# Attention with the causal mask added in VectorE's copy of diagonal blocks, one full unit in four split by GpSimd, and new ranks in the planner

## The chip, the cores and the metric

One core of a Trainium2 chip. The metric is the device time of one execution in microseconds (us). Engines: TensorE (PE, its weight loads PEld), VectorE (DVE), ScalarE (ACT), GpSimd (POOL), SyncE (SP), which issues most DMAs.

## What is computed

One step of a hybrid encoder layer over 2048 prompt rows and 64 decode rows (with 128 cached keys), 8 heads of 64, all in float32:

```python
s = jnp.einsum('bqhd,bkhd->bhqk', q, k) * sc
s = s + (Fi[:, :, :, None] - Ft[:, :, None, :])      # F: running sum of log gates
s = jnp.where(kpos[None, :] <= qpos[:, None], s, -jnp.inf)
pr = jax.nn.softmax(s, axis=-1)
attn = jnp.einsum('bhqk,bkhd->bqhd', pr, v)
z = jnp.concatenate([attn * silu(ag), pool * silu(pg)], axis=-1)
y = rmsnorm(x + gate * (z @ w_out), final_g)
```

Ahead of it stand a normalization, one projection to q, k, v, gates and pooling inputs, and a pooling mixer. The last two lines above are what follows the attention.

## The kernel before

`stage_project` (to about 620 us) makes q, k, v, gates and pooling and leaves them in DRAM. `stage_finish` does the attention (620 to about 1075 us) and the output projection.

**Attention.** For each of 8 heads there are three steps: query groups c = 0 and 1 together (and the decode rows), c = 2, c = 3, where a group is 512 query rows. A step's `score` blocks are 128 query rows by up to 512 keys: TensorE makes a block by two matmuls (L1456, L1457), and for a row's last block a third, the mask (L1459), an identity times a triangular tile, both bf16. VectorE copies the block to `wts` and takes its maximum (L1571), and after a row's last block the negated maximum of the row (L1576). ScalarE takes the exponential in place, with its sum (L1528). A `unit` is 128 keys by 512 queries (fewer on the diagonal), 42 a head: `turn`, up to four fp32 transposes on TensorE (L1472); `high`, ScalarE's rounding to fp32r (L1534); `low`, VectorE's remainder (L1581); `value`, two matmuls of v with both halves (L1487). At an output's last unit ScalarE takes one half of the bank (`out`, L1542), and VectorE adds the other (`add`, L1589). A step's denominators are inverted by VectorE (`den`, L1601). In a head the outputs are c = 0, the decode rows, c = 1, 2, 3, five in all; units 0 to 3 belong to c = 0, 4 and 5 to decode, 6 to 13 to c = 1, 14 to 25 to c = 2 and 26 to 41 to c = 3. Heads run one behind the other, counted from 0.

**Rings.** Score banks 3 (`S_RING`), transpose banks 3 (`T_RING`: a bank is free after `low`), `whi` and `wlo` 6 (`W_RING`: `high` of unit i waits for `value` of unit i - 6), output banks 2. The copies of a step wait for the last transposes of two steps before.

**Order.** The instructions of TensorE, ScalarE and VectorE stand in an order that `Plan.run` writes at build time: again and again it takes the operation that can begin first by its table of costs, and by `PRIORITY` where two could begin together. Each kind keeps its own order. On the chip an engine executes its list in this order.

**Gates.** For the odd head of a pair, GpSimd multiplies each output of both heads by its gate and by the inverse denominators: `g_mul` (L1645), then `g_hi`, `g_z`, `g_lo` (L1650, L1651, L1654), four operations for each of 5 outputs. `g_mul` waits for `ag` and for `rb`, the inverse denominators of both heads repeated over partitions. These go by DRAM: `rec_out` (L1352) writes them to `rden`, `gate_in` (L1361) waits for that and loads `ag` and `rb`, two buffers each, so the third output's load waits for the first's `g_lo`. In SyncE's one queue stand between these: the load of the next head's v (it waits for the last `value` of the step before), the load of q and k of the head after next once a head's last score is made, and the stores of z (they wait for `g_lo`). GpSimd has nothing else to do in the attention:

```python
for out in OUTS:
    if out.step.e == 0: continue
...
    pool.wait_ge(rb_in[n % 2], 48 * (n // 2 + 1))
    pool.tensor_tensor(a, a, r, ALU.mult).then_inc(g_mul, 1)
    pool.wait_ge(out_ok, out.i + 1)
```

Near the end of the attention ScalarE and VectorE also split w_out in eight slices (`w_high`, `w_low`, L1563).

## Time and profile before

| | |
|---|---|
| time, median of 3 runs | 1275.52 us (1273.33 to 1277.78) |
| the profiled execution | 1271.05 us, its span 1269.3 us |
| granted clock of TensorE, mean | 0.992 |
| busy: PE, DVE, ACT, POOL | 97%, 56%, 44%, 15% of the span |
| instructions: PE, DVE, ACT, POOL | 7039, 1969, 1158, 193 |

The page gives busy times over the span, which averages stages with different limits: the projection (TensorE full, VectorE light), the attention, and the output projection. The table of busy times in short stretches separates them. In a line of the order of time, the first number is the start in us from the span's start, the second the duration, then engine, line, operation, out <- in with shapes, and in brackets the idle time of the engine before it with what ended it. Matmuls overlap in their pipeline, so the distance of two starts is their price, not their duration.

### The profile page before, as it was taken

To read this page: it belongs to the slowest core of one execution; us is meant where nothing else is said; L and a number is where in the kernel's file an instruction comes from. 1 tells how busy PE (TensorE), PEld (TensorE's weight loads), DVE (VectorE), ACT (ScalarE), POOL (GpSimd) and SP (SyncE) were. 2 spreads that over 40 slices of the span, in tenths; PEclk is the share of its full clock that TensorE was granted. 3 is DMA by queue.
4 is the path that set the end of the run, shared out by engine and by line. 5 is a ranking of instruction groups with operands and counts; after the bars stand their busy time and mean duration, and the time that the engine had idled before them with its cause. 6 is when DMAs were issued, how large, how long until landed. Compare 5 with 4: busy or idle time off the path is not lost. (4 is left out here: it accounts for less than half of the span.)

```text
span 1269.3 us, 19390 instructions
## 1 busy us (share of the span) xinstructions
PE 1229.5 (97%) x7039; PEld 1025.5 (81%) x7039; DVE 710.4 (56%) x1969; ACT 563.1 (44%) x1158; POOL 184.4 (15%) x193
## 2 busy tenths in 40 slices
PE   4899999999999999999999999999999998999997
PEld 1799988888888888888878778778787886888884
DVE  1856433334564121110069899999899998444444
ACT  3757321222121112211168789887788877101111
POOL 1433301010010000101000051032123114100000
PEclk8899999999999999999999999999999999999999
DMA  9855454022122444337175859948877965766662
GB/s 370 323 176 189 138 149 141 34 69 83 36 85 69 142 141 140 112 127 179 52 168 47 149 89 159 129 119 147 121 129 123 115 177 168 212 189 196 199 199 67
DMA packets 161893, 179.52 MB, mean 141 GB/s; under 512 B 34773, under 2 KB 124249, under 8 KB 157638
## 3 DMA queue, kind: packets, MB, share of 16 engines
q1 hardware_dynamic: 157030, 160.97, 50.9%
q10 hardware_dynamic: 4768, 17.30, 4.1%
q8 instruction: 57, 0.93, 0.4%
q14 instruction: 38, 0.31, 0.1%
HBM read 111.55 MB, written 66.69 MB: 140 GB/s over the span
## 5 line engine op out<-in xcount | busy, mean ns | idle before, releaser
L617 PE MATMUL prj_acc<-prj_hhi,til_whi 128*128 128x512 f32 (+1 forms) x800 | 285.9, 357 | 0.0
L618 PE MATMUL prj_acc<-prj_hhi,til_wlo 128*128 128x512 f32 (+1 forms) x800 | 284.8, 356 | 0.0
L619 PE MATMUL prj_acc<-prj_hlo,til_whi 128*128 128x512 f32 (+1 forms) x800 | 283.7, 355 | 0.0
L1571 DVE TENSOR_SCALAR_CACHE_REDUCE att_wts<-att_sps 128x512 f32<-128x512 f32 (+4 forms) x328 | 186.4, 595 | 89.8 <-PE att_sps L1459 88.9
L1581 DVE TENSOR_TENSOR att_wlo<-att_tps,att_whi 128x512 fp32r<-128x512 f32 (+1 forms) x336 | 183.3, 583 | 16.6 <-ACT att_whi L1534 15.9
L1534 ACT ACTIVATE att_whi<-att_tps 128x512 fp32r<-128x512 f32 (+1 forms) x336 | 160.7, 515 | 51.1 <-PE att_tps L1472 27.1
L1528 ACT ACTIVATE att_wts<-att_wts,att_nm 128x1024 f32<-128x1024 f32 (+8 forms) x200 | 175.2, 880 | 14.7 <-DVE att_nm L1576 12.6
L617 PEld LDWEIGHTS prj_acc<-prj_hhi,til_whi 128*128 128x128 f32 x800 | 150.5, 188 | 21.9
L619 PEld LDWEIGHTS prj_acc<-prj_hlo,til_whi 128*128 128x128 f32 x800 | 150.5, 188 | 21.6
L618 PEld LDWEIGHTS prj_acc<-prj_hhi,til_wlo 128*128 128x128 f32 x800 | 150.6, 188 | 21.1
L1472 PE MATMUL att_tps<-keep_ident,att_wts 128*128 128x128 f32 x1088 | 158.3, 275 | 7.0 <-DVE att_wlo L1581 5.5
L1472 PEld LDWEIGHTS att_tps<-keep_ident,att_wts 128*128 128x128 f32 x1088 | 124.6, 141 | 36.4 <-issue 18.2
L1487 PE MATMUL att_ops<-att_whi,att_vt 128*128 128x512 f32 (+1 forms) x336 | 136.0, 409 | 0.6 <-DVE att_att L1589 0.3
L1487 PE MATMUL att_ops<-att_wlo,att_vt 128*128 128x512 f32 (+1 forms) x336 | 119.5, 363 | 0.0
L977 DVE SCALAR_TENSOR_TENSOR til_olo<-prj_acc,til_ohi 128x512 fp32r<-128x512 f32 (+1 forms) x40 | 23.8, 597 | 153.3 <-ACT til_ohi L800 153.3
L530 POOL TENSOR_TENSOR til_wlo<-til_wraw,til_whi 128x1024 fp32r<-128x1024 f32 x20 | 48.1, 2403 | 410.1 <-ACT til_whi L726 410.1
L1549 ACT ACTIVATE zin_junk<-zin_y 128x1024 bf16<-128x1024 f32 (+1 forms) x17 | 18.0, 1058 | 157.2 <-DVE zin_y L1615 157.2
L1645 POOL TENSOR_TENSOR att_ag<-att_ag,att_rb 128x512 f32<-128x512 f32 (+1 forms) x20 | 22.1, 1104 | 393.4 <-DMA att_rb<-scratch_rden 393.4
L1487 PEld LDWEIGHTS att_ops<-att_whi,att_vt 128*128 128x128 f32 x336 | 64.8, 193 | 8.8 <-DVE att_wlo L1581 2.1
L1487 PEld LDWEIGHTS att_ops<-att_wlo,att_vt 128*128 128x128 f32 x336 | 64.4, 192 | 4.2
L1456 PE MATMUL att_sps<-keep_ka,keep_qa 128*128 128x512 f32 (+4 forms) x164 | 65.8, 401 | 1.7 <-PEq L203 1.5
L1456 PE MATMUL att_sps<-att_ka,att_qa 128*128 128x512 f32 (+4 forms) x164 | 65.9, 402 | 0.0
(188 smaller groups left out, 1854.5 us busy)
## 6 DMA issues: line engine op xcount, KB each, us to landing
til_wraw<-in_w_in SPq DMA_DIRECT2D x20, 512.0 KB, 4.2
scratch_v<-val_vs SPq DMA_DIRECT2D x17, 512.0 KB, 4.8
val_xt<-in_x_prompt ACTq DMA_DIRECT2D x16, 512.0 KB, 4.5
ini_al<-in_w_ada SPq DMA_DIRECT2D x8, 1024.0 KB, 15.3
zin_zh<-scratch_z SPq DMA_DIRECT2D x16, 512.0 KB, 4.3
zin_zl<-scratch_z SPq DMA_DIRECT2D x16, 512.0 KB, 5.7
zin_xr<-in_x_prompt SPq DMA_DIRECT2D x16, 512.0 KB, 5.4
out_y_prompt<-zin_o ACTq DMA_DIRECT2D x16, 512.0 KB, 2.7
```

The costliest lines, as they stand in the source:

```text
L530: pool.tensor_tensor(wlo[t.n % 2][:, :, :], wraw[:, :, :], raw(whi[t.n % 2][:, :, :]), ALU.subtract).then_inc(wt_lo, 1)
L617: pe.matmul(out, w[0][:, k, :], hhi[:, k, cs], start=(k == 0), stop=False)
L618: pe.matmul(out, w[1][:, k, :], hhi[:, k, cs], start=False, stop=False)
L619: mm = pe.matmul(out, w[0][:, k, :], hlo[:, k, cs], start=False, stop=(k == KT - 1))
L977: dve.scalar_tensor_tensor(out=olo[use.slot][:, 0:x.n], in0=acc[x.i % ACC_RING][:, 0:x.n], scalar=SCALE if x.tile.kind == "Q" else 1.0, in ...
L1456: pe.matmul(bank[0:x.m, 0:x.n], qa[e][:, q], ka[e][:, k], start=True, stop=False)
L1472: mm = pe.transpose(bank[:, t * P:(t + 1) * P], weights(st, 4 * x.c + t, x.w0, P), keep["ident"][:, :])
L1487: mm = pe.matmul(bank[:, x.skip:x.width], vt[e][0:x.keys, x.tile, :], part[b][0:x.keys, x.skip:x.width], start=(x.first and part is whi), ...
L1528: act.activation(w, w, ACT.Exp, bias=nm[0:x.m, e, x.row:x.row + 1], accum_out=den[0:x.m, e, x.row, x.part:x.part + 1]).then_inc(exp_ok, 1)
L1534: act.activation(whi[x.i % W_RING][0:x.keys, x.skip:x.width], tps[x.i % T_RING][0:x.keys, x.skip:x.width], ACT.Copy).then_inc(hi_ok, 1)
L1571: dve.tensor_scalar(weights(st, x.row, x.w0, x.n), sps[x.i % S_RING][0:x.m, 0:x.n], 1.0, None, ALU.mult, ALU.max, accum_out=top[0:x.m, e, ...
L1581: dve.tensor_tensor(wlo[b][0:x.keys, x.skip:x.width], tps[x.i % T_RING][0:x.keys, x.skip:x.width], raw(whi[b][0:x.keys, x.skip:x.width]), ...
```

## The change

- The mask's matmul and its bf16 identity are gone. The mask is a float32 tile of 64 + 4 x 128 columns, zero but for two triangles, built by GpSimd behind its last normalization work of the projection. VectorE's copy of a row's last block is a `tensor_tensor_reduce` that adds a slice of it and takes the maximum.
- Of full units (no decode, nothing skipped) those with i % 4 == 3, 52 in all, are split by GpSimd: ScalarE copies the transposes as float32 to one of two new buffers `wf`, GpSimd copies these to `whi` (`p_high`) and writes the remainder to `wlo` (`p_low`); the bank is free after ScalarE. `value` waits for `p_ok`.
- GpSimd gets an order from the planner as well, in which these two and the four gate operations stand; `g_mul` is ready in the plan at the later of the output's `add` and `den` + 9 us. In the plan every GpSimd operation costs 1150 ns.
- TensorE's ranks are turn, value, score, with the score's rank by how many of the last scores are not yet copied; the costs of TensorE's matmuls are higher in the plan.

```diff
-MASKED = -1e30
+MASKED, LOWEST = -1e30, -3e38
...
-            pool.memset(keep["mask"][:, :], 0.0).then_inc(const, 1)
-            pool.affine_select(out=keep["mask"][:, :], in_=keep["mask"][:, :], compare_op=ALU.is_ge, fill=MASKED,
-            pool.wait_ge(const, 6)
-            pool.tensor_copy(keep["identb"][:, :], ident[:, :]).then_inc(const, 1)
...
+            pool.wait_ge(sq, NT)
+            pool.memset(keep["mask"][:, :], 0.0).then_inc(masked, 1)
+            pool.wait_ge(masked, 1)
+            for c0, n in ((0, DEC), (DEC + 3 * P, P)):
+                pool.affine_select(out=keep["mask"][:, c0:c0 + n], in_=keep["mask"][:, c0:c0 + n], compare_op=ALU.is_ge, fill=MASKED,
+                                   base=0, pattern=[[-1, n]], channel_multiplier=1).then_inc(masked, 1)
...
+F_UNITS = 2
+POOL_UNITS = [u.i for u in UNITS if u.i % 4 == 3 and not u.dec and not u.skip]
+GATED = [out for out in OUTS if out.step.e == 1]
+GATE_LAG = 9000
+def dve_units(i):
+    return i + 1 - sum(j <= i for j in POOL_UNITS)
...
-    PRIORITY = {"PE": ("turn", "score", "value"), "ACT": ("out", "high", "exp", "w_high"), "DVE": ("low", "add", "score", "den", "w_low")}
+    PRIORITY = {"PE": ("turn", "value", "score"), "ACT": ("out", "high", "exp", "w_high"), "DVE": ("low", "add", "score", "den", "w_low"),
+                "POOL": ("p_high", "p_low", "g_lo", "g_z", "g_hi", "g_mul")}
-        self.free = {"PE": 0, "ACT": 0, "DVE": 0}
-        self.order = {"PE": [], "ACT": [], "DVE": []}
+        self.free = {"PE": 0, "ACT": 0, "DVE": 0, "POOL": 0}
+        self.order = {"PE": [], "ACT": [], "DVE": [], "POOL": []}
-        self.tables = {"turn": UNITS, "value": UNITS, "high": UNITS, "low": UNITS, "out": OUTS, "add": OUTS, "exp": PIECES, "den": STEPS,
+        self.tables = {"turn": UNITS, "value": UNITS, "high": UNITS, "out": OUTS,
+                       "low": [u for u in UNITS if u.i not in POOL_UNITS], "p_high": [UNITS[i] for i in POOL_UNITS],
+                       "p_low": [UNITS[i] for i in POOL_UNITS], "g_mul": GATED, "g_hi": GATED, "g_z": GATED, "g_lo": GATED, "add": OUTS, "exp": PIECES, "den": STEPS,
+    def turned(self, i):
+        return self.at("high" if i in POOL_UNITS else "low", i)
+    def halved(self, i):
+        return self.at("p_low" if i in POOL_UNITS else "low", i)
...
-            return max(at("exp", LAST_PIECE[x.i]), at("low", x.i - T_RING))
+            return max(at("exp", LAST_PIECE[x.i]), self.turned(x.i - T_RING))
-            return max(at("low", x.i), at("add", x.out.i - O_RING) if x.first else 0, self.arrived(x, x.c))
+            return max(self.halved(x.i), at("add", x.out.i - O_RING) if x.first else 0, self.arrived(x, x.c))
+            if x.i in POOL_UNITS:
+                r = POOL_UNITS.index(x.i)
+                return max(at("turn", x.i), at("p_low", POOL_UNITS[r - F_UNITS]) if r >= F_UNITS else 0)
+        if kind == "p_high":
+            return max(at("high", x.i), at("value", x.i - W_RING))
+        if kind == "g_mul":
+            return max(at("add", x.i), at("den", x.step.index) + GATE_LAG)
+        if kind in ("p_low", "g_hi", "g_z", "g_lo"):
+            return at({"p_low": "p_high", "g_hi": "g_mul", "g_z": "g_hi", "g_lo": "g_z"}[kind], x.i)
...
-            mask = 50 if kind == "score" and x.last else 0
-            return 24 + 6 * x.n // 7 + mask + (80 if self.short else 0), 200
+            return 24 + 9 * x.n // 10 + (80 if self.short else 0), 200
+        if engine == "POOL":
+            return 1150, 100
...
+    def rank(self, engine, kind, x, t):
+        if engine != "PE" or kind != "score":
+            return self.PRIORITY[engine].index(kind)
+        waiting = sum(self.at("copied", i) > t for i in range(max(0, x.i - S_RING), x.i))
+        return -1 if waiting < 1 else 0.5 if waiting < 2 else 2
...
-                    key = (begin, self.PRIORITY[engine].index(kind))
+                    key = (begin, self.rank(engine, kind, table[n], begin))
-                self.short = kind == "turn" or (kind == "score" and x.last)
+                self.short = kind == "turn"
...
+def mask_of(x):
+    at = 0 if x.row == NQ else DEC + 3 * P - x.mask0
+    return slice(at, at + x.n)
...
-                    mm = pe.matmul(bank[0:x.m, 0:x.n], qb[e][:, q], kb[e][:, k], start=False, stop=not x.last)
-                    if x.last:
-                        mm = pe.matmul(bank[0:x.m, x.mask0:x.mask0 + x.m], keep["identb"][0:x.m, 0:x.m],
-                                       keep["mask"][0:x.m, 0:x.m], start=False, stop=True)
+                    mm = pe.matmul(bank[0:x.m, 0:x.n], qb[e][:, q], kb[e][:, k], start=False, stop=True)
-                    if x.i >= T_RING:
-                        pe.wait_ge(lo_ok, x.i - T_RING + 1)
+                    if x.i - T_RING in POOL_UNITS:
+                        pe.wait_ge(hi_ok, x.i - T_RING + 1)
+                    elif x.i >= T_RING:
+                        pe.wait_ge(lo_ok, dve_units(x.i - T_RING))
...
                         pe.wait_ge(v_in[e], V * (h // 2 + e))
                     if x.first and x.out.i >= O_RING:
                         pe.wait_ge(out_ok, x.out.i - O_RING + 1)
-                    pe.wait_ge(lo_ok, x.i + 1)
+                    if x.i in POOL_UNITS:
+                        pe.wait_ge(p_ok, POOL_UNITS.index(x.i) + 1)
+                    else:
+                        pe.wait_ge(lo_ok, dve_units(x.i))
                     bank = ops[x.out.i % O_RING]
                     b = x.i % W_RING
                     for part in (whi, wlo):
...
-            pe.wait_ge(lo_ok, NU)
+            pe.wait_ge(lo_ok, dve_units(NU - 1))
...
+                elif kind == "high" and x.i in POOL_UNITS:
+                    r = POOL_UNITS.index(x.i)
+                    act.wait_ge(t_full, x.i + 1)
+                    if r >= F_UNITS:
+                        act.wait_ge(p_ok, r - F_UNITS + 1)
+                    act.activation(wf[r % F_UNITS][:, :], tps[x.i % T_RING][:, :], ACT.Copy).then_inc(hi_ok, 1)
...
-                    dve.tensor_scalar(weights(st, x.row, x.w0, x.n), sps[x.i % S_RING][0:x.m, 0:x.n],
-                                      1.0, None, ALU.mult, ALU.max,
-                                      accum_out=top[0:x.m, e, x.row, x.b:x.b + 1]).then_inc(s_free, 1)
-                    if x.last:
+                    w, src, most = weights(st, x.row, x.w0, x.n), sps[x.i % S_RING][0:x.m, 0:x.n], top[0:x.m, e, x.row, x.b:x.b + 1]
+                    if not x.last:
+                        dve.tensor_scalar(w, src, 1.0, None, ALU.mult, ALU.max, accum_out=most).then_inc(s_free, 1)
+                    else:
+                        dve.tensor_tensor_reduce(w, src, keep["mask"][0:x.m, mask_of(x)], 1.0, LOWEST, ALU.add, ALU.max,
+                                                 accum_out=most).then_inc(s_free, 1)
...
-            for out in OUTS:
...
+            for kind, x in ORDER["POOL"]:
+                if kind in ("p_high", "p_low"):
+                    r, b = POOL_UNITS.index(x.i), x.i % W_RING
+                    if kind == "p_high":
+                        pool.wait_ge(hi_ok, x.i + 1)
+                        if x.i >= W_RING:
+                            pool.wait_ge(val_ok, x.i - W_RING + 1)
+                        pool.tensor_copy(whi[b][:, :], wf[r % F_UNITS][:, :]).then_inc(p_hi, 1)
+                    else:
+                        pool.wait_ge(p_hi, r + 1)
+                        pool.tensor_tensor(wlo[b][:, :], wf[r % F_UNITS][:, :], raw(whi[b][:, :]), ALU.subtract).then_inc(p_ok, 1)
+                n, cols = gates(x), x.cols
+                hi, lo = zhi[n % 2][:, 0:x.width], zlo[n % 2][:, 0:x.width]
+                a, r = ag[n % 2][:, 0:x.width], rb[n % 2][:, 0:x.width]
+                if kind == "g_mul":
+                    pool.wait_ge(rb_in[n % 2], 48 * (n // 2 + 1))
+                    pool.tensor_tensor(a, a, r, ALU.mult).then_inc(g_mul, 1)
+                elif kind == "g_hi":
+                    pool.wait_ge(out_ok, x.i + 1)
+                    pool.wait_ge(g_mul, n + 1)
+                    if n >= 2:
+                        pool.wait_ge(z_out[n % 2], 32 * (n // 2))
+                    pool.tensor_tensor(hi, a, att[:, cols], ALU.mult).then_inc(g_hi, 1)
+                elif kind == "g_z":
+                    pool.wait_ge(out_ok, x.i + 1)
+                    pool.wait_ge(g_mul, n + 1)
+                    pool.tensor_tensor(r, a, att[:, cols], ALU.mult).then_inc(g_z, 1)
+                else:
+                    pool.wait_ge(g_hi, n + 1)
+                    pool.wait_ge(g_z, n + 1)
+                    pool.tensor_tensor(lo, r, raw(hi), ALU.subtract).then_inc(g_lo, 1)
```

## Rows read from the trace of the kernel before

**Rows 1.** one stretch by engine: busy us, instructions, granted clock, DMA.

```profile
860.00:920.00 60.00, 59.30 (x364) 47.84 (x363) 55.23 (x169) 48.85 (x109) 6.79 (x6) 1.00 0.83 135
```

**Rows 2.** groups by shape, 700 to 1040 us: count, busy us, mean ns.

```profile
L1571 DVE TENSOR_SCALAR_CACHE_REDUCE att_wts<-att_sps 128x512 f32<-128x512 f32 x180 | 118.3, 681 | 0.7 <-PE att_tps L1472 0.5
L1581 DVE TENSOR_TENSOR att_wlo<-att_tps,att_whi 128x512 fp32r<-128x512 f32 x180 | 116.1, 682 | 15.5 <-ACT att_whi L1534 15.1
L1650 POOL TENSOR_TENSOR att_zhi<-att_ag,att_att 128x512 fp32r<-128x512 f32 x12 | 15.4, 1286 | 1.6
L1650 POOL TENSOR_TENSOR att_zhi<-att_ag,att_att 128x64 fp32r<-128x64 f32 x4 | 1.3, 321 | 0.5
```

**Rows 3.** TensorE in time (start us, us, line): a mask, then transposes.

```profile
805.31 0.23 PE L1459 MATMUL att_sps<-keep_mask,keep_identb 128*128 128x128 bf16 x1
805.38 0.61 PE L1472 MATMUL att_tps<-keep_ident,att_wts 128*128 128x128 f32 x4
```

**Rows 4.** VectorE in time: denominators (L1601), outputs' adds (L1589).

```profile
804.40 0.18 DVE L1601 RECIPROCAL att_rec<-att_den 128x8 f32<-128x8 f32 x1
819.04 0.69 DVE L1589 TENSOR_TENSOR att_att<-att_ops,att_tmp 64x512 f32<-64x512 f32 x1
867.34 0.70 DVE L1589 TENSOR_TENSOR att_att<-att_ops,att_tmp 64x512 f32<-64x512 f32 x1
910.22 0.18 DVE L1601 RECIPROCAL att_rec<-att_den 128x8 f32<-128x8 f32 x1
```

**Rows 5.** GpSimd in time: first gate operation, head 3's first, last output.

```profile
832.36 1.30 POOL L1645 TENSOR_TENSOR att_ag<-att_ag,att_rb 128x512 f32<-128x512 f32 x1 [45.48 <-DMA att_rb<-scratch_rden]
886.63 1.29 POOL L1645 TENSOR_TENSOR att_ag<-att_ag,att_rb 128x512 f32<-128x512 f32 x1 [24.82 <-DMA att_rb<-scratch_rden]
```

**Rows 6.** SyncE's queue in time: gate loads of the same two outputs.

```profile
826.69 0.35 SPq L1369 DMA_DIRECT2D att_ag<-scratch_ag  x1
864.08 0.34 SPq L1369 DMA_DIRECT2D att_ag<-scratch_ag  x1
```

**Rows 7.** TensorE's values: units 7, 13 of head 3; 1, 7 of head 4.

```profile
821.49 0.48 PE L1487 MATMUL att_ops<-att_whi,att_vt 128*128 128x512 f32 x1
830.15 0.40 PE L1487 MATMUL att_ops<-att_whi,att_vt 128*128 128x512 f32 x1
869.39 0.34 PE L1487 MATMUL att_ops<-att_whi,att_vt 128*128 128x384 f32 x1
875.23 0.48 PE L1487 MATMUL att_ops<-att_whi,att_vt 128*128 128x512 f32 x1
```

**Rows 8.** add and first gate operation: heads 1, 5 (last), 7 (first).

```profile
761.49 0.69 DVE L1589 TENSOR_TENSOR att_att<-att_ops,att_tmp 64x512 f32<-64x512 f32 x1
781.48 1.29 POOL L1645 TENSOR_TENSOR att_ag<-att_ag,att_rb 128x512 f32<-128x512 f32 x1 [23.62 <-DMA att_rb<-scratch_rden]
973.25 0.69 DVE L1589 TENSOR_TENSOR att_att<-att_ops,att_tmp 64x512 f32<-64x512 f32 x1
993.92 1.29 POOL L1645 TENSOR_TENSOR att_ag<-att_ag,att_rb 128x512 f32<-128x512 f32 x1 [24.00 <-DMA att_rb<-scratch_rden]
1030.78 0.69 DVE L1589 TENSOR_TENSOR att_att<-att_ops,att_tmp 64x512 f32<-64x512 f32 x1
1042.42 1.29 POOL L1645 TENSOR_TENSOR att_ag<-att_ag,att_rb 128x512 f32<-128x512 f32 x1 [43.10 <-DMA att_rb<-scratch_rden]
```

**Rows 9.** TensorE after idle near the attention's end; those 10 us.

```profile
1071.08 1.09 PE L1472 MATMUL att_tps<-keep_ident,att_wts 128*128 128x128 f32 x4 [1.81 <-DVE att_wlo L1581]
1070.00:1080.00 10.00, 8.92 (x35) 7.45 (x36) 6.82 (x9) 1.86 (x3) 1.47 (x1) 0.83 0.64 175
```

**Rows 10.** VectorE, low halves of w_out: alone, and beside a GpSimd operation.

```profile
1063.25 1.21 DVE L1563 TENSOR_TENSOR olo_w<-raw_w,ohi_w 128x1024 fp32r<-128x1024 f32 x1
1068.24 2.09 DVE L1563 TENSOR_TENSOR olo_w<-raw_w,ohi_w 128x1024 fp32r<-128x1024 f32 x1
```

**Rows 11.** GpSimd's one copy with one input, by shape.

```profile
L518 POOL CAST keep_identb<-keep_ident 128x128 bf16<-128x128 f32 x1 | 0.3, 289 | 0.1
```

More of the change, by code:

```diff
@@ L18 @@
 PAST = 128
+MASK_COLS = DEC + 4 * P
 HEADS = 8
@@ L227, in stage_project @@
             hf = a.sb("hf", [P, 2, D])
-            junk = a.sb("junk", [P, D], BF16)
+            junk = keep["junk"]
             vf = a.sb("vf", [P, 2, 512])
@@ L260, in stage_project @@
         names = ("wt_in", "wt_hi", "wt_lo", "full", "free_a", "free_d", "split_hi", "kf_ok", "m_done", "m_free", "wp_in", "wp_ok",
-                 "early_ok", "ck_in", "sp_in", "f_step", "f_exp", "f_ok", "f_hi", "f_part", "f_out",
+                 "early_ok", "masked", "ck_in", "sp_in", "f_step", "f_exp", "f_ok", "f_hi", "f_part", "f_out",
                  "d_step", "d_ok", "z_hi", "z_lo", "fill")
         (wt_in, wt_hi, wt_lo, full, free_a, free_d, split_hi, kf_ok, m_done, m_free, wp_in, wp_ok,
-         early_ok, ck_in, sp_in, f_step, f_exp, f_ok, f_hi, f_part, f_out,
+         early_ok, masked, ck_in, sp_in, f_step, f_exp, f_ok, f_hi, f_part, f_out,
          d_step, d_ok, z_hi, z_lo, fill) = (s.sem(f"t_{n}") for n in names)
@@ L575, in _ @@
             pe.wait_ge(rows_in, 80)
-            pe.wait_ge(const, 4)
+            pe.wait_ge(const, 3)
             pe.transpose(ada[0][:, 0:NROWS], rows[:, :], ident[0:NROWS, 0:NROWS]).then_inc(turned, 1)
@@ L1278, in stage_finish @@
         wlo = [s.sb(f"wlo{n}", [P, 512], F32R) for n in range(W_RING)]
+        wf = [s.sb(f"wf{n}", [P, 512]) for n in range(F_UNITS)]
         top = s.sb("top", [P, 2, NR, 4])
@@ L1294, in stage_finish @@
         names = ("s_full", "s_free", "row_ok", "exp_ok", "t_full", "hi_ok", "lo_ok", "val_ok", "low_out", "out_ok",
-                 "den_sum", "rec_ok", "g_mul", "g_hi", "g_z", "g_lo")
+                 "den_sum", "rec_ok", "p_hi", "p_ok", "g_mul", "g_hi", "g_z", "g_lo")
         (s_full, s_free, row_ok, exp_ok, t_full, hi_ok, lo_ok, val_ok, low_out, out_ok,
-         den_sum, rec_ok, g_mul, g_hi, g_z, g_lo) = (s.sem(n) for n in names)
+         den_sum, rec_ok, p_hi, p_ok, g_mul, g_hi, g_z, g_lo) = (s.sem(n) for n in names)
         rd_out, rb_in, z_out = ([s.sem(f"{n}{e}") for e in range(2)] for n in ("rd_out", "rb_in", "z_out"))
@@ L1636, in _ @@
         def _(pool):
-            for out in OUTS:
-                if out.step.e == 0:
-                    continue
-                pair, cols = out.step.pair, out.cols
-                n = gates(out)
-                hi, lo = zhi[n % 2][:, 0:out.width], zlo[n % 2][:, 0:out.width]
-                a, r = ag[n % 2][:, 0:out.width], rb[n % 2][:, 0:out.width]
-                pool.wait_ge(rb_in[n % 2], 48 * (n // 2 + 1))
-                pool.tensor_tensor(a, a, r, ALU.mult).then_inc(g_mul, 1)
-                pool.wait_ge(out_ok, out.i + 1)
-                pool.wait_ge(g_mul, n + 1)
-                if n >= 2:
-                    pool.wait_ge(z_out[n % 2], 32 * (n // 2))
-                pool.tensor_tensor(hi, a, att[:, cols], ALU.mult).then_inc(g_hi, 1)
-                pool.tensor_tensor(r, a, att[:, cols], ALU.mult).then_inc(g_z, 1)
-                pool.wait_ge(g_hi, n + 1)
-                pool.wait_ge(g_z, n + 1)
-                pool.tensor_tensor(lo, r, raw(hi), ALU.subtract).then_inc(g_lo, 1)
+            for kind, x in ORDER["POOL"]:
[9 more added lines that the diff above has]
+                        pool.tensor_tensor(wlo[b][:, :], wf[r % F_UNITS][:, :], raw(whi[b][:, :]), ALU.subtract).then_inc(p_ok, 1)
+                    continue
+                n, cols = gates(x), x.cols
[18 more added lines that the diff above has]
+                    pool.tensor_tensor(lo, r, raw(hi), ALU.subtract).then_inc(g_lo, 1)
@@ L1672, in build @@
         keep = {
-            "ident": s.sb("ident", [P, P]), "identb": s.sb("identb", [P, P], BF16), "mask": s.sb("mask", [P, P], BF16),
+            "ident": s.sb("ident", [P, P]),
             "cols": s.sb("cols", [P, NROWS]),
@@ L1676, in build @@
         }
+        with Scope(nc, "sqr") as a:
+            keep["junk"] = a.sb("junk", [P, D], BF16)
+        keep["mask"] = s.sb("mask", [P, MASK_COLS])
         with Scope(nc, "val") as a:
```

3 lines of the change are left out of this document (1 added, 2 removed).

## Prediction

> **What bounds the kernel now.** I first read the page's 40 slices: TensorE is full everywhere at full clock, and the stretch from slice 20 to slice 34 (about 620 to 1070 us, 447 us) is the attention, the only part whose work the change touches. The busy time by stretch of that stage [rows 1] shows TensorE at 59.3 of 60 us, VectorE at 55.2, ScalarE at 48.9 and GpSimd at 6.8. A busy TensorE is not a TensorE at its peak, so I compared two denominators of the same stage, VectorE's sum of row softmax to row softmax [rows 4]: from the one of head 3 (804.40) to that of head 5 (910.22) two heads take 105.8 us, 52.9 us each. VectorE is busy 92% of this, so 48.7 us a head. TensorE and VectorE are both nearly full, in queues whose order is written out by the planner: work taken from both should shorten a head. But in such queues one instruction that waits holds everything behind it, so I looked next at what GpSimd waits for. Today it does only the gates, and each time its first multiply (the line of `g_mul`) starts long after the attention output that it belongs to is there [rows 4, 5, 8]. Today nobody waits for that. This is what the prediction turns on.
>
> **Taken from TensorE: the mask matmul.** 16 rows and one decode row a head, 136 in all. The mask starts at 805.31 and the transposes behind it at 805.38 [rows 3]: 0.07 us each, and at most about 0.15 us if the long matmul behind it pays a start as well. That is 17 x 0.07 to 0.15 = 1.2 to 2.6 us a head.
>
> **Moved to VectorE: the mask in the copy.** The diagonal copies change from a scalar operation with a maximum to `tensor_tensor_reduce`. No row shows that operation. The nearest are a copy of 512 columns, 681 ns, and a tensor_tensor of 512 from PSUM and SBUF, 682 ns [rows 2]: no difference. I take nothing, as its two inputs lie where those of `low` lie. The bounds: slightly below nothing (1 us a head), if the maximum is written without an instruction of its own, and a second pass over the block: the mean diagonal block has 312 columns, 312/512 x 0.68 = 0.42 us, so 17 x 0.42 = 7 us a head more.
>
> **Taken from VectorE: the low halves of 52 units.** Units with i % 4 == 3, full and not decode, are 7 in an even head (units 7, 11, 15, 23, 27, 31, 39 of its 42) and 6 in an odd one (13, 17, 25, 29, 33, 41). Each spares a tensor_tensor of 0.68 us, some 0.6 us as they follow each other: 4 us a head of VectorE's 48.7. ScalarE is unchanged, as it writes `wf` in place of `whi`.
>
> **Added on GpSimd.** Each of the 52 units costs a copy and a subtraction. The subtraction is 1.29 us [rows 2]. The copy has no row at this size; a cast of 128 columns took 0.29 us [rows 11]. A two-input operation of 64 columns takes 0.32 and one of 512 1.29 [rows 2], so 0.18 is fixed; with that the cast's rate puts 512 columns at 0.18 + 4 x 0.11 = 0.6; the upper bound is the two-input 1.29. I take 0.6. So 52 x 1.9 = 99 us on an engine with 85% free; its load is no problem, its order is.
>
> **The order on GpSimd.** The new queue holds `p_high` and `p_low` among the gates. The planner makes `g_mul` ready at the later of the output's add and denominator + 9 us. Measured, denominator + 9 is 813.4 and the add of head 3's first output is at 819.04 [rows 4]: the add decides, and `g_mul` is put right behind it. But its `rb` rows come over DRAM: SyncE issues their load at 826.69 only [rows 6], and `g_mul` starts at 832.36 [rows 5], 28.0 us behind the denominator and 13.3 behind the add. In the new queue everything behind it stands still until then. What stands behind? The next GpSimd unit of an odd head is 13; `p_high` needs the value matmuls of unit 7 (ring of 6), which start at 821.49 [rows 7], after the add. So it can't be put ahead. Its own value matmul starts at 830.15 [rows 7]. In the new kernel it needs: 832.4 + g_mul 1.3 + the decode part's g_mul (its loads are issued behind the first's, so I put it at an end of about 835.3) + g_hi 1.3 + copy 0.6 + one gate operation between the two 1.3 + subtraction 1.3 = 840.1. TensorE stands still for **10 us**.
>
> The last output of an odd head is the same: its add is at 867.34 [rows 4], its loads are issued at 864.08 [rows 6] behind the whole q and k load of the next odd head, and `g_mul` starts at 886.63 [rows 5], 19.3 us late. Behind it stands unit 7 of the next head, which needs the value of unit 1 (869.39, again after the add) and whose value matmul starts at 875.23 [rows 7]. SyncE's chain moves by 3.4 us only. It waits for the decode part's last gate: before at 832.4 + 4 x 1.3 + 4 x 0.4 = 839.2, now at 840.1 + 1.3 + 3 x 0.4 = 842.6 (an estimate; the order of the four gate operations and the unit's two isn't shown). The landing is then at 890.0, and the value matmul can start at 890.0 + 1.3 + 1.3 + 0.6 + 1.3 + 1.3 = 895.8, in place of 875.2. The two middle outputs are less late and I give them nothing, as the next unit behind each comes later.
>
> **The sum for one pair of heads.** Denominator of head 3 to value of unit 13: 840.1 - 804.4 = 35.7 us (25.8 before). To the value of unit 7 in the next head: 895.8 - 840.1 = 55.7 us (45.1 before). From there to the next such denominator 910.22 - 875.23 = 35.0 us, less 3.6% for the lighter engines (1.9 us a head, the middle of the mask's 1.2 to 2.6, as TensorE is the fuller one), 33.7, and one restart of TensorE at the low clock. After an idle time of 1.8 us it was granted 0.83 of the clock over 10 us [rows 9], that is 3.4 us at 1.2 in place of 2.4 GHz and 1.7 us of work lost. Sum 35.7 + 55.7 + 33.7 + 1.7 = 126.8 us against 105.8: **21 us more a pair**. The pairs of heads 1 and 2, and 5 and 6, have the same lateness (last output 20.0 and 20.7 us) [rows 8]; I take the same 21 for each. Head 7 has only the first: 11.6 us late [rows 8], so 8.3 + 1.7 = 10 us. Head 0 and the rest of head 7 gain 3.6% of some 80 us, 3 us. The end costs 2 us (below). Sum 3 x 21 + 10 - 3 + 2 = 72 us. The profiled run took 1271.05 us (its span is 1269.3), the median of the three is 1275.5, 4.5 above. 1275.5 + 72 gives **1347 us**.
>
> **At the end of the attention** the eight low halves of w_out, VectorE reading two SBUF inputs, run beside GpSimd: 1.21 us alone, 2.09 us beside a GpSimd operation [rows 10]. Head 7's last units 29, 33 and 41 add six GpSimd operations there: at most 6 x 0.9 = 5 us, partly beside other work; I took 2. The Trainium skill says in SBUF: State Buffer, Who interferes with whom, that a VectorE instruction with two SBUF inputs and a GpSimd one that reads SBUF exclude each other, the later blocking fully, and that one SBUF input doesn't contend. The trace agrees with the first (2.09 against 1.21). By it the masked copy, with PSUM and one SBUF input, doesn't slow. The sum is the same by the row.
>
> **Edits that cost nothing.** The mask is built later on GpSimd, two selects and a fill, under 2 us at a point where that engine waits for ScalarE for most of the projection; if this cover were gone it would cost these 2 us. The bf16 identity goes. The ranks of the plan let score matmuls wait when two scores are not yet copied; a step's copies wait for the transposes of two steps before, so denominators can't come much earlier, and a later one only makes the gates later.
>
> **The rivals.** (a) *No blocking*, the gates' loads are there in time. Then a head goes from 52.9 to about 51.0 us, as TensorE loses 1.9 and VectorE 4: 8 x 1.9 = 15 us, **1260 us**, faster. For it: both full engines get lighter. Against it: lateness of 11.6 to 20.7 us [rows 8] and four more such places, on a chain of SyncE and DMA that the change leaves alone. It decides if the loads land within some 2 us of the add. Chance 0.17. (b) *Half the blocking*: DMA queues run emptier while TensorE waits, or the order saves one of the two units: 36 us, **1311 us**. The unit after is needed only 3 to 6 us later, which takes that much from each wait. Chance 0.12. (c) *The masked copy takes two passes* and there is no blocking: VectorE has 7 - 4 = 3 us more a head, 51.7, about what TensorE and it together take now: **1275 us**, no change. Chance 0.04. The forecast keeps 0.67. Together with (c) its own range is 1325 to 1372: the copy on GpSimd at 1.29 adds 0.7 x 7 = 5 us, the masked copy at two passes up to 20 in all (3 us a head, less in the waits), and shorter waits at each of seven places (3 us) take 20.
>
> **How the numbers follow.** What a measurement of this kernel can tell from no change is about 0.3%, 4 us. Slower: 0.67 + 0.12 = 0.79; within: 0.04; faster: 0.17. To hold 8 in 10 the range goes from 1272 (no change, and half the blocking) to 1375.
>
> **What would show it.** Right: GpSimd's longest waits are still for the load of `rb`, and now TensorE's value line waits for GpSimd's `p_low`, seven times 8 to 20 us, with the clock below 1 in these places; two heads take some 126 us; VectorE's busy time falls by about 31 us. Wrong: no wait of TensorE over 3 us in the attention and two heads under 103 us (then the loads land in time, and a); or copies with the mask well over 0.7 us (c).

## The result and the profile after

The changed kernel takes 1350.2 us (median; 1348.1 to 1354.8), 1.060 times the kernel before (95% interval 1.057 to 1.062), which took 1275.4. It is 75 us slower. Its profiled execution, the slowest of four, has a span of 1353.1 us, 83.8 above the 1269.3 of the profile before. For run e7 below, one execution in a slower state is left out of the median, and its profile isn't used. From the changed kernel's page, the span, the busy times, and TensorE, VectorE and the granted clock in 40 slices:

```profile
span 1353.1 us, 19241 instructions
PE 1236.3 (91%) x6903; PEld 1040.6 (77%) x6903; DVE 686.9 (51%) x1917; ACT 564.3 (42%) x1158; POOL 282.3 (21%) x297
PE   4999999999999999999996989688968967999997
DVE  1856323443561211100885868586857867344444
PEclk8899999999999999999897989798978998999999
```

TensorE lost a tenth or more in half of the slices of the attention, and in most of these its clock is lower too. The waits of the whole execution (who waited for whom; us in total, times, longest):

```profile
POOL att_whi L1700 <- ACT att_wf L1583: 193.3, 32, 56.2
POOL att_ag L1710 <- DMA att_rb<-scratch_rden: 167.8, 17, 26.7
PE att_ops L1535 <- POOL att_wlo L1703: 76.4, 10, 13.4
DVE att_att L1645 <- ACT att_tmp L1596: 56.8, 12, 13.7
```

GpSimd waited in all less for its gate loads than before, and now TensorE waits behind it: 76.4 us in 10 waits, most of the 83.8 us between the two profiled executions. TensorE in order of time, the seven waits over 5 us:

```profile
735.75 0.80 PE L1535 MATMUL att_ops<-att_whi,att_vt 128*128 128x512 f32 x1 [12.08 <-POOL att_wlo L1703]
789.67 0.79 PE L1535 MATMUL att_ops<-att_whi,att_vt 128*128 128x512 f32 x1 [6.44 <-POOL att_wlo L1703]
862.62 0.80 PE L1535 MATMUL att_ops<-att_whi,att_vt 128*128 128x512 f32 x1 [13.41 <-POOL att_wlo L1703]
919.48 0.80 PE L1535 MATMUL att_ops<-att_whi,att_vt 128*128 128x512 f32 x1 [8.93 <-POOL att_wlo L1703]
991.22 0.80 PE L1535 MATMUL att_ops<-att_whi,att_vt 128*128 128x512 f32 x1 [12.29 <-POOL att_wlo L1703]
1045.14 0.80 PE L1535 MATMUL att_ops<-att_whi,att_vt 128*128 128x512 f32 x1 [6.12 <-POOL att_wlo L1703]
1115.06 0.80 PE L1535 MATMUL att_ops<-att_whi,att_vt 128*128 128x512 f32 x1 [10.18 <-POOL att_wlo L1703]
```

The first, third, fifth and seventh are the first outputs of heads 1, 3, 5 and 7 (12.1, 13.4, 12.3, 10.2 us), the others the last outputs of heads 1, 3 and 5 (6.4, 8.9, 6.1). The one at 862.62, on GpSimd in order of time, with the last output's first gate operation behind the dots, answers to [rows 5]:

```profile
856.22 1.26 POOL L1710 TENSOR_TENSOR att_ag<-att_ag,att_rb 128x512 f32<-128x512 f32 x1 [26.75 <-DMA att_rb<-scratch_rden]
858.03 0.32 POOL L1710 TENSOR_TENSOR att_ag<-att_ag,att_rb 128x64 f32<-128x64 f32 x1 [0.55 <-DMA att_rb<-scratch_rden]
858.30 1.26 POOL L1716 TENSOR_TENSOR att_zhi<-att_ag,att_att 128x512 fp32r<-128x512 f32 x1
859.51 0.61 POOL L1700 CAST att_whi<-att_wf 128x512 fp32r<-128x512 f32 x1
860.08 1.26 POOL L1720 TENSOR_TENSOR att_rb<-att_ag,att_att 128x512 f32<-128x512 f32 x1
861.30 1.26 POOL L1703 TENSOR_TENSOR att_wlo<-att_wf,att_whi 128x512 fp32r<-128x512 f32 x1
...
913.78 1.26 POOL L1710 TENSOR_TENSOR att_ag<-att_ag,att_rb 128x512 f32<-128x512 f32 x1 [15.46 <-DMA att_rb<-scratch_rden]
```

`g_mul` of the first output comes when its load is there, then the decode part's, `g_hi`, the copy of unit 13 at 859.51, a gate operation, the remainder at 861.30, and at 862.62 TensorE goes on. VectorE's denominators and the add of the same output answer to [rows 4]:

```profile
825.41 0.18 DVE L1657 RECIPROCAL att_rec<-att_den 128x8 f32<-128x8 f32 x1
840.49 0.83 DVE L1645 TENSOR_TENSOR att_att<-att_ops,att_tmp 64x512 f32<-64x512 f32 x2
...
955.15 0.18 DVE L1657 RECIPROCAL att_rec<-att_den 128x8 f32<-128x8 f32 x1
```

Two heads take 955.15 - 825.41 = 129.7 us (105.8 before). SyncE's loads for the same two outputs answer to [rows 6]:

```profile
849.58 0.35 SPq L1415 DMA_DIRECT2D att_ag<-scratch_ag  x1
890.69 0.34 SPq L1415 DMA_DIRECT2D att_ag<-scratch_ag  x1
```

After the waits TensorE runs at the lower clock. The busy times of the stretch of [rows 1], of ten of its microseconds from just ahead of the end of the wait, and of shorter stretches around two restarts:

```profile
860.00:920.00 60.00, 47.17 (x269) 38.87 (x270) 41.61 (x130) 39.78 (x88) 30.16 (x32) 0.90 0.73 120
860.00:870.00 10.00, 7.38 (x35) 6.33 (x36) 3.92 (x11) 4.18 (x9) 7.21 (x10) 0.64 0.39 112
860.00:862.50 2.50, 0.00 (x0) 0.00 (x0) 0.00 (x0) 0.00 (x0) 2.50 (x3) 0.50 0.00 0
862.50:865.00 2.50, 2.38 (x10) 2.08 (x10) 0.50 (x1) 0.86 (x2) 2.50 (x6) 0.50 0.14 52
865.00:867.50 2.50, 2.50 (x10) 2.03 (x9) 1.78 (x5) 1.67 (x4) 1.42 (x2) 0.56 0.95 311
920.00:925.00 5.00, 5.00 (x19) 4.24 (x18) 2.67 (x6) 1.78 (x5) 2.45 (x2) 0.50 0.67 120
925.00:930.00 5.00, 5.00 (x30) 4.42 (x30) 3.69 (x15) 4.19 (x8) 1.89 (x2) 0.98 0.06 2
```

The granted clock is 0.64 in 860 to 870 and 0.90 over the 60 us. It is 0.50 (1.2 of 2.4 GHz) already in the idle time ahead of 862.62, which costs nothing, and stays there until about 867.2: 4.6 us of work at half speed, 2.3 us lost. Behind the restart at 919.48 it stays until about 925.2, 2.9 us lost. (Both ends are estimates from the means 0.56 and 0.98 of the last stretches.) The new operations:

```profile
L1629 DVE CUSTOM_DVE_ANT_0 att_wts<-att_sps,keep_mask 128x512 f32<-128x512 f32 x32 | 21.9, 684 | 89.2 <-PE att_sps L1503 89.0
L1629 DVE CUSTOM_DVE_ANT_0 att_wts<-att_sps,keep_mask 128x256 f32<-128x256 f32 x32 | 13.3, 417 | 0.3
L1700 POOL CAST att_whi<-att_wf 128x512 fp32r<-128x512 f32 x52 | 34.1, 656 | 197.5 <-ACT att_wf L1583 193.3 <-PE att_ops L1535 4.2
```

The masked copy takes what the plain copy took [rows 2], 684 and 681 ns; GpSimd's copy takes 0.66 us in the mean. The columns are as in [rows 1] and [rows 2].

### The profile page after: what moved, and what is told of

Read it like the earlier page. It is cut to its first block and busy times, and to the rows that moved or that the text cites. A ratio compares the mean times of both kernels' runs of the same rounds, so it can differ in the third digit from the quotient of the medians.

```text
span 1353.1 us, 19241 instructions
## 1 busy us (share of the span) xinstructions
PE 1236.3 (91%) x6903; PEld 1040.6 (77%) x6903; DVE 686.9 (51%) x1917; ACT 564.3 (42%) x1158; POOL 282.3 (21%) x297
## 5 line engine op out<-in xcount | busy, mean ns | idle before, releaser
L1535 PE MATMUL att_ops<-att_whi,att_vt 128*128 128x512 f32 (+1 forms) x336 | 135.7, 408 | 76.4 <-POOL att_wlo L1703 76.4
L1637 DVE TENSOR_TENSOR att_wlo<-att_tps,att_whi 128x512 fp32r<-128x512 f32 (+5 forms) x284 | 152.5, 567 | 42.8 <-ACT att_whi L1588 42.5
L1517 PE MATMUL att_tps<-keep_ident,att_wts 128*128 128x128 f32 x1088 | 165.5, 286 | 8.4 <-DVE att_wlo L1637 7.7
L1517 PEld LDWEIGHTS att_tps<-keep_ident,att_wts 128*128 128x128 f32 x1088 | 132.1, 147 | 46.8 <-issue 28.5
L1588 ACT ACTIVATE att_whi<-att_tps 128x512 fp32r<-128x512 f32 (+5 forms) x284 | 135.6, 502 | 74.0 <-PE att_ops L1535 38.4
L1627 DVE TENSOR_SCALAR_CACHE_REDUCE att_wts<-att_sps 128x512 f32<-128x512 f32 x192 | 127.6, 684 | 18.4 <-PE att_sps L1503 14.6
L1535 PE MATMUL att_ops<-att_wlo,att_vt 128*128 128x512 f32 (+1 forms) x336 | 122.3, 373 | 0.0
L1629 DVE CUSTOM_DVE_ANT_0 att_wts<-att_sps,keep_mask 128x512 f32<-128x512 f32 (+4 forms) x136 | 64.5, 475 | 90.3 <-PE att_sps L1503 89.6
L1700 POOL CAST att_whi<-att_wf 128x512 fp32r<-128x512 f32 x52 | 34.1, 656 | 197.5 <-ACT att_wf L1583 193.3
```

The source lines that it names most:

```text
L1517: mm = pe.transpose(bank[:, t * P:(t + 1) * P], weights(st, 4 * x.c + t, x.w0, P), keep["ident"][:, :])
L1535: mm = pe.matmul(bank[:, x.skip:x.width], vt[e][0:x.keys, x.tile, :], part[b][0:x.keys, x.skip:x.width], start=(x.first and part is whi), ...
L1588: act.activation(whi[x.i % W_RING][0:x.keys, x.skip:x.width], tps[x.i % T_RING][0:x.keys, x.skip:x.width], ACT.Copy).then_inc(hi_ok, 1)
L1627: dve.tensor_scalar(w, src, 1.0, None, ALU.mult, ALU.max, accum_out=most).then_inc(s_free, 1)
L1629: dve.tensor_tensor_reduce(w, src, keep["mask"][0:x.m, mask_of(x)], 1.0, LOWEST, ALU.add, ALU.max, accum_out=most).then_inc(s_free, 1)
L1637: dve.tensor_tensor(wlo[b][0:x.keys, x.skip:x.width], tps[x.i % T_RING][0:x.keys, x.skip:x.width], raw(whi[b][0:x.keys, x.skip:x.width]), ...
```

## The experiments

The theory on trial: the time is lost because GpSimd, in order, stands at a gate's first multiply until its load has landed, with halves of units behind it that TensorE needs. The rivals: the split itself (its longer way, its load), the ranks, the masked copy. Times are medians, beside the ratio to the kernel before on the same chip with its 95% interval; "a pair" is the distance of the first denominators of heads 3 and 5 in the profiled execution, one execution of each kernel.

### Late gates (e1)

```diff
-            return max(at("add", x.i), at("den", x.step.index) + GATE_LAG)
+            n = GATED.index(x)
+            lag = 42000 if x.step.index % NG == NG - 1 else 31000
+            return max(at("add", x.i), at("den", x.step.index) + lag, at("g_lo", GATED[n - 2].i) + 8000 if n >= 2 else 0)
```

> Same instructions as the changed kernel, only the order written for GpSimd (and by it, slightly, the others) differs: in the plan a gate's first multiply is ready 31 us after its step's denominators (42 us for the last output of a head) and 8 us after the gate two before it, as the trace of the kernel before shows the loads to land. Theory (the queue behind the load of rb is what costs the time): no wait of TensorE for GpSimd over 3 us, two heads in about 102 us, 1255 to 1268 us. Rival (the split itself costs it: a longer chain per unit, or GpSimd and VectorE in each other's way): the waits stay, at every unit of GpSimd's, and the time stays above 1300 us.

Measured 1286.4 us, 1.0084 [1.0053, 1.0116], a pair 106.4 us. The longest wait of TensorE for GpSimd's half is 2.9 us. So the order alone is worth 64 of the 75 us, and the split as such isn't what costs the most. But the expected gain over the kernel before (1255 to 1268 us) isn't there: the time lies between theory and rival.

### The same order, no gate loads (e8)

```diff
-                sp.dma_start(ag[n % 2][:, 0:out.width], dram["ag"][st.pair, :, out.cols]).then_inc(rb_in[n % 2], 16)
-                for e in range(2):
-                    sp.dma_start(rb[n % 2][halves(e)[0], 0:out.width],
-                                 dram["rden"][2 * st.pair + e, out.cols].partition_broadcast(DH)).then_inc(rb_in[n % 2], 16)
...
-                    pool.wait_ge(rb_in[n % 2], 48 * (n // 2 + 1))
-                    pool.tensor_tensor(a, a, r, ALU.mult).then_inc(g_mul, 1)
+                    pool.tensor_tensor(a, a, a, ALU.mult).then_inc(g_mul, 1)
```

> The changed kernel instruction for instruction in its own order, but the loads of ag and rb are left out and the gates' first multiply works on ones that are filled in once (it squares them), so it waits for no DMA; attention isn't gated or divided by its denominators in what is stored. Theory (it is that wait, not the order or the work): TensorE's waits for GpSimd's half go, as in e1: 1280 to 1290 us. Rival (gates in the way by their own 20 operations of 1.29 us): 1300 us or more.

Measured 1275.7 us, 0.9996 [0.9973, 1.0019], a pair 104.8 us (802.53 to 907.32). This kernel leaves out the gates' values and the division by the denominators. It has the changed kernel's own order with all its operations on the engines, and without the loads and the wait it is as fast as the kernel before: they are worth the whole 75 us, and the time is below the theory's 1280 to 1290. Between the two profiled executions there are 83.9 us (1353.1 less 1269.2). TensorE is busy 1236.3 us in the one and 1215.4 in the other with the same 6903 matmuls, so 20.9 us of this are matmuls that take longer, with the clock of the restarts above as the likely reason, and 63.0 are idle time. TensorE's waits from 640 to 1100 us:

```profile
PE att_tps L1513 <- DVE att_wlo L1633: 10.3, 20, 1.4
PE att_ops L1531 <- POOL att_wlo L1702: 6.2, 7, 2.0
```

6.2 us for GpSimd's halves in 7 waits, in place of 76.

### Only the last outputs late (e6)

```diff
-            return max(at("add", x.i), at("den", x.step.index) + GATE_LAG)
+            lag = 42000 if x.step.index % NG == NG - 1 else GATE_LAG
+            return max(at("add", x.i), at("den", x.step.index) + lag)
```

> The changed kernel with only the last output's gate of each odd head placed late in GpSimd's order (42 us behind its denominators in the plan); the first output's stays right behind its add. Theory (two separate standstills a pair, about 13 us for the last output and 13 for the first): 3 waits go and 4 stay, two heads in about 115 us, 1310 to 1322 us. Rival (one wait takes the place of the other, since the chain of loads ends when it ends): above 1335 us.

Measured 1328.5 us, 1.0415 [1.0377, 1.0452], a pair 117.1 us: 22 us less than the changed kernel for three waits taken away. The four first outputs' waits stay:

```profile
736.81 0.80 PE L1536 MATMUL att_ops<-att_whi,att_vt 128*128 128x512 f32 x1 [14.77 <-POOL att_wlo L1704]
854.97 0.79 PE L1536 MATMUL att_ops<-att_whi,att_vt 128*128 128x512 f32 x1 [13.42 <-POOL att_wlo L1704]
972.56 0.80 PE L1536 MATMUL att_ops<-att_whi,att_vt 128*128 128x512 f32 x1 [13.98 <-POOL att_wlo L1704]
1089.98 0.80 PE L1536 MATMUL att_ops<-att_whi,att_vt 128*128 128x512 f32 x1 [11.43 <-POOL att_wlo L1704]
```

The two standstills are separate. Three waits with 21.5 us of idle time are gone, and the first ones grew by 5.6 us in all (14.8, 13.4, 14.0 and 11.4 us). All of TensorE's waits for GpSimd fell from 76.4 to 61.6 us, and its busy time from 1236.3 to 1225.3: the 22 us are idle time and slower matmuls together. The time is 6.5 us over the theory's range and as much under the rival's bound.

### Mask alone (e3), ranks and mask (e2)

```diff
-POOL_UNITS = [u.i for u in UNITS if u.i % 4 == 3 and not u.dec and not u.skip]
+POOL_UNITS = []
```

This is e2. e3 has in addition `PRIORITY` of TensorE, the cost 24 + 6n/7 and the rank by the table, as before the change.

> Mask in VectorE's copy alone, on the old ranks and the old matmul costs of the plan, no unit split by GpSimd. Theory: 136 mask matmuls at 0.07 to 0.15 us leave TensorE, VectorE's load is the same: 1258 to 1270 us, TensorE-bound stretches shorter by 1 to 2.5 us a head. Rival (masked copy dearer on the engine that bounds): 1275 us or more.

> The changed kernel with no unit split by GpSimd: mask in the copy and new ranks alone. GpSimd holds only gates again, which wait for the same loads, but nothing stands behind them. Theory: 1260 to 1272 us, the mask's 10 to 20 us on TensorE less what VectorE, with its low halves back, can't follow. Rival (ranks or masked copy cost part of the 75 us): above 1280 us.

e3 measured 1275.5 us, 1.0005 [0.9983, 1.0026], a pair 105.7 us. e2 measured 1285.9 us, 1.0087 [1.0059, 1.0115], a pair 109.1 us. Both came out as their rivals had it. The mask's 136 matmuls leave TensorE, and nothing is gained. Where its time went: the busy times from 700 to 1000 us of the kernel before, then of e3,

```profile
700.00:1000.00 300.00, 297.44 (x1811) 238.31 (x1810) 279.45 (x859) 247.69 (x546) 64.93 (x60) 1.00 0.76 129
```

```profile
700.00:1000.00 300.00, 290.94 (x1716) 233.16 (x1715) 278.76 (x851) 247.59 (x544) 63.79 (x60) 1.00 0.79 131
```

and TensorE's waits from 640 to 1100 us, first before, then e3:

```profile
PEld att_sps L1456 <- DVE att_wts L1571: 7.8, 28, 0.5
PEld att_tps L1472 <- ACT att_wts L1528: 2.5, 8, 0.5
```

```profile
PEld att_sps L1502 <- DVE att_wts L1627: 11.0, 38, 0.5
PEld att_tps L1517 <- ACT att_wts L1576: 9.7, 22, 2.5
PE att_ops L1535 <- DVE att_att L1645: 5.8, 6, 1.1
```

TensorE is busy 6.5 us less in 300 and idle that much more; over the attention its waits for copies, exponentials and adds grew. VectorE is busy 279 of 300 in both. In this comparison TensorE's time was free. The order of e3 isn't quite that of the kernel before, since its plan has no cost for the mask.

### The mask's matmul put back at a fixed order (e9), VectorE's time put back (e10)

Both are e8 with these lines.

```diff
-                    mm = pe.matmul(bank[0:x.m, 0:x.n], qb[e][:, q], kb[e][:, k], start=False, stop=True)
+                    mm = pe.matmul(bank[0:x.m, 0:x.n], qb[e][:, q], kb[e][:, k], start=False, stop=not x.last)
+                    if x.last:
+                        zero = [keep["mask"][0:x.m, DEC + 64 * n:DEC + 64 * n + 64].bitcast(BF16)[:, 0:x.m] for n in range(2)]
+                        mm = pe.matmul(bank[0:x.m, x.mask0:x.mask0 + x.m], zero[0], zero[1], start=False, stop=True)
```

> e8_no_gate_loads (the changed kernel in its own order, the gates waiting for no load) with 136 matmuls of zeros by zeros of the mask's shape put back on TensorE, at each row's last block. It tells what the mask matmul is worth at a fixed order, with VectorE already relieved. Theory P (TensorE bounds there): 0.07 to 0.15 us each, 10 to 20 us more than e8 (1275.7), some 1290 us; two heads from 104.8 to 107 us or more. Theory V (VectorE, its order and the hand-overs bound): under 4 us more.

```diff
+    if _kind == "low" and _x.i - 1 in POOL_UNITS:
+        MORE.append(("more", _x))
...
+                if kind == "more":
+                    dve.tensor_reduce(spare[:, POOL_UNITS.index(x.i - 1):POOL_UNITS.index(x.i - 1) + 1], keep["mask"][:, DEC:], AX, ALU.max)
```

> e8_no_gate_loads with 51 more operations on VectorE that wait for nothing (a maximum over 512 columns of zeros, some 0.6 us each), one ahead of the low half that follows each GpSimd unit: the time of the low halves taken over by GpSimd is put back on VectorE at a fixed order. Theory V (VectorE bounds): most of 51 x 0.6 = 30 us shows, 1295 us or more. Theory P (TensorE bounds, VectorE has room): under 8 us more than e8 (1275.7).

e9 measured 1273.9 us, 0.9995 [0.9979, 1.0011], a pair 104.2 us: nothing beside e8. (Its profiled execution took 1281.4 us, so the pair says less than the median.) e10 measured 1293.8 us, 1.0156 [1.0142, 1.0170], a pair 110.1 us: 18 us over e8. Its added operations (count | busy, mean ns):

```profile
L1618 DVE TENSOR_REDUCE att_spare<-keep_mask 128x1 f32<-128x512 f32 x51 | 34.5, 677 | 0.2
```

34.5 us of operations more on VectorE (its whole busy time rose by 28.9, 686.7 to 715.6, as neighbours overlap) cost 18 us. TensorE's waits for VectorE's low halves rose from 10.3 to 23.6 us, while GpSimd's halves took 1.28 us as before, so they weren't in each other's way. At this order added time on VectorE costs half to two thirds of itself and the mask on TensorE nothing. The rival (under 8 us) is out; the theory that VectorE bounds had asked for 1295 us or more, most of the 30 us, and is missed by one.

### The split with old ranks (e4), the split alone (e7), and the old ranks without loads (e12)

e4 is e1 with the ranks and costs of e3. e7 is e4 with the mask on TensorE as before. e12 is e8 with the ranks and costs of e3:

```diff
-    PRIORITY = {"PE": ("turn", "value", "score"),
+    PRIORITY = {"PE": ("turn", "score", "value"),
...
-            return 24 + 9 * x.n // 10 + (80 if self.short else 0), 200
+            return 24 + 6 * x.n // 7 + (80 if self.short else 0), 200
...
-        if engine != "PE" or kind != "score":
+        if True:
```

> As e1_late_gates (gates placed late, 52 units split by GpSimd, mask in the copy), but with the ranks and matmul costs of the kernel before. Theory (ranks are worth little): within 6 us of e1_late_gates. Rival (ranks carry the gain): 8 us or more above it.

> As e4_split_old_ranks but with the mask back on TensorE (bf16 identity times triangle) and the plain copy with a maximum on VectorE: the split alone, with late gates and the old ranks. The mask alone gave no change (e3). Theory V (VectorE and its order bound a head, TensorE's mask time was free): as e4 within 0.4%, about 1278 us. Theory P (TensorE bounds once VectorE is relieved): 8 us or more above e4, 1286 us.

> e8_no_gate_loads with the ranks and matmul costs of the plan of the kernel before (the gates again wait for no load and work on ones). So far the ranks cost 8 us with the split (e1 against e4) and 10 us without (e2 against e3), the mask is worth nothing on TensorE (e3, e9), and VectorE's time is worth 18 us for 51 operations (e10). Theory (the split's relief of VectorE is a gain that the ranks take away): 8 us or more under e8, 1263 to 1268 us. Rival (the relief is lost in the longer way of a unit over GpSimd, ranks or not): within 4 us of 1275.

e4 measured 1278.4 us, 1.0032 [1.0011, 1.0053], 8 us under e1, and a pair is 103.7 us, 2.1 less than before. That is neither of its two theories (within 6 us of e1, or 8 or more above). e7 measured 1293.6 us (1291.1, 1293.6 and 1301.0), 1.0154 [1.0115, 1.0192]: 15 us above e4. That is what its theory P asked for, 8 us or more if TensorE bounds once VectorE is relieved, and against e9. e12 measured 1286.0 us, 1.0076 [1.0052, 1.0100], a pair 108.0 us. So the old ranks are 8 us better with late gates (e1 to e4), 10 us better without a split (e2 to e3) and 10 us worse here (e8 to e12). An effect with both signs isn't one of the ranks alone: a newly written order can fall out some 10 us better or worse, and neither theory of e12 stands. That bounds what e3 and e4 say of their parts, and may be part of e7's 15 us, since putting the mask back there also rewrote the order; how much wasn't separated.

### Last head or last pair without GpSimd units (e5, e11)

```diff
-POOL_UNITS = [u.i for u in UNITS if u.i % 4 == 3 and not u.dec and not u.skip]
+POOL_UNITS = [u.i for u in UNITS if u.i % 4 == 3 and not u.dec and not u.skip and u.step.head < HEADS - 1]
```

e5 is e4 with this, e11 with `HEADS - 2`. What they are to mend, TensorE of e4 at the end of the attention:

```profile
1075.10 0.80 PE L1537 MATMUL att_ops<-att_whi,att_vt 128*128 128x512 f32 x1 [7.75 <-POOL att_wlo L1705]
1081.18 0.77 PE L1556 MATMUL att_sps<-ohi_w,zin_zh 128*128 128x512 f32 x1 [4.85 <-DMA zin_zl<-scratch_z]
```

> e4_split_old_ranks with no GpSimd unit in the last head (46 units in all in place of 52). In e4 two heads took 103.9 us in place of 105.8, and it gave that back at the end: TensorE waited 7.8 us for a GpSimd half behind the last gates and 4.9 us for the first z rows. Theory (order at the end): both waits go, 1266 us (1263 to 1270). Rival (the gain a head isn't real and the end is the load of w_out's low halves): 1275 us or more.

> Late gates, old ranks, mask in the copy, and GpSimd units in heads 0 to 5 only (39 units), so that the last pair's chain from denominators over gates to the first z rows runs as in the kernel before. Theory (two heads of the split order save 1.9 us, and the loss of e4 and e5 is all in the last pair): three pairs save 6 us and the end costs nothing, 1269 us. Rival (what the order saves is lost again wherever the split stops): 1275 us or more.

e5 measured 1278.7 us, 1.0024 [1.0002, 1.0046], e11 1282.6 us, 1.0072 [1.0057, 1.0086]; both miss their theories (1266 and 1269 us) and lie where their rivals had them (1275 or more). In e11 TensorE waits at the start of the output projection:

```profile
PE att_sps L1556 <- DMA zin_zl<-scratch_z: 11.9, 1, 11.9
```

The heads run ahead, but the chain from the denominators over the gates to the first z rows doesn't, and the saved time is waited for at its end. No version was faster than the kernel before.

## Why the prediction was right, and where not

**The mechanism was right**, as put in the order on GpSimd: `g_mul` behind the add, the load later, the next unit's halves behind it. e8 takes away that wait, together with its loads, and gives back all 75 us; e1 keeps wait and loads, puts the gates later in the order, and gives 64.

**The terms for a pair** (heads 3 and 5): denominator to value of unit 13, forecast 35.7 us, measured 862.62 - 825.41 = 37.2; from there to unit 7 of the next head 55.7, measured 919.48 - 862.62 = 56.9; from there to the next denominator with its restart 33.7 + 1.7, measured 955.15 - 919.48 = 35.7. In all 129.7 for 126.8; the other two pairs took 125.8 and 126.0. The load landed 30.8 us behind the denominators (856.22 - 825.41) in place of 28.0. Behind it the order was the one assumed, and GpSimd took 6.4 us from `g_mul` to TensorE's start where 7.7 were forecast (the terms listed there add up to 839.8, not 840.1). Head 7's first output: 10.2 us of idle time for 8.3. The end: 4.4, 0.5 and 2.0 us of waits for GpSimd, for 2 forecast. Total 75 us for 72.

**Luck in the total.** The 75 us are between medians; between the two profiled executions, from which the terms are read, it is 83.8. The three pairs gave 65.3 of these (316.2 us became 381.5; forecast 63), and 18.8 came behind head 7's first denominators (253.2 us became 272.0), where the forecast had 12 less a part of its 3 us of gain. The profiled execution before lay 4.3 us under its median and the one after 4.6 above. So the pairs were forecast well, and the end by some 8 us too low.

**Sizes that were off.** The forecast called for seven waits of 8 to 20 us; they were 6.1 to 13.4, as the first wait moves the add as well, and so takes from the second's lateness: the last output's add is at 902.76 and its load is there at 913.78, 11.0 us for 19.3 before. The restart at the low clock was taken as 1.7 us and counted once a pair; there are two, of 2.3 and 2.9 us. The first lies ahead of a load that decides when the next wait ends. The second should show in the last term, which yet grew only from 35.0 to 35.7 us; what covered the rest wasn't separated. VectorE's busy time fell by 23.5 us (710.4 to 686.9), not 31.

**The step that failed is the gain**: "TensorE is the fuller one", so 1.9 us a head. It is in rival (a), which the prediction priced at 1260 us. e8 is that case, and it took 1275.7, with 104.8 us a pair for 105.8: 0.5 us a head. The mask's matmul is worth nothing in e3 beside the kernel before and in e9 beside e8 (within 0.2%), while time added to VectorE costs half or more of itself (e10). Only e7 beside e4 has it otherwise, by 15 us and with a new order. So that TensorE is the fuller one isn't borne out at a fixed order, and not excluded for every order. In the sum itself this term was small (3 us, and 1.3 a pair), so it hardly moved the total.

**Rival (b)**, half the blocking, has one of the two waits left. e6 is that case with 1328.5 us: it costs 53 us, not the 36 of the prediction. **Rival (c)**, two passes of the masked copy: excluded by 684 against 681 ns.

**Left open.** 52 low halves of 0.68 us left VectorE. If time taken from it were worth what added time costs (e10), that would be some 15 to 18 us (an estimate); e8 still isn't faster than before. Its three pairs are 2.5 us shorter (313.7 for 316.2), and 3.9 us are lost behind head 7's denominators (257.1 for 253.2). Some of it are waits for low halves (10.3 us in e8, 5.5 before) and for GpSimd (6.2 us). What the rest is, and why an order falls out 10 us better or worse (e12 against e8), wasn't separated.

## What to carry to other kernels

Before work that others need is put into the queue of an idle engine, look at what that engine waits for: a wait that cost nothing becomes a wait for everything behind it, and here the load came 11.6 to 20.7 us behind the add at the five places read from the trace before. A plan that places such an operation needs the time at which its data land on the chip, from the trace, not a round figure. And "busy 99%" didn't say whose time counts: at one fixed order (e8, from 700 to 1000 us) TensorE was busy 97% and VectorE 89%, and it was VectorE's, which only adding work to the one and then to the other showed (e9, e10). Where an edit rewrites the order, 10 us of 1275 say nothing of the edit itself.

## What the runs showed of the hardware

The two-input copy with a mask and a maximum (`tensor_tensor_reduce` from PSUM and SBUF) runs at the speed of the one-input copy with a maximum: 684 against 681 ns at 512 columns, 417 against 414 at 256, with a separate read of the accumulator of 82 ns in both. GpSimd's float32 copy of 128 x 512 takes 0.61 us alone (0.66 in the mean, up to 1.6 beside the low halves of w_out), half of its two-input operation of 1.29 us.

In all of the changed kernel's attention no two-input operation of GpSimd on a half of a unit was held up by VectorE (minimum, median and maximum in ns, first and last start):

```profile
L1703 POOL TENSOR_TENSOR att_wlo<-att_wf,att_whi x52: 1262/1286/1302, 660.7 to 1155.2; 128x512 fp32r<-128x512 f32 x52
```

The masked copy and the low halves of turned weights read one input from PSUM and one from SBUF, and the longest of GpSimd's 52 remainders took 1302 ns, for the 1286 ns in the mean of such an operation before [rows 2].

The Trainium skill says in SBUF: State Buffer, Who interferes with whom, that a VectorE instruction with at most one SBUF input, outside the modes that use both of its ports, doesn't contend with GpSimd. The trace agrees: 1262 to 1302 ns.
